# A conv FFN on one core: loads, squares and conversions put at other steps of the down projection

## The reference, cut to what matters

```python
h = rms_norm(x, norm_ffn)
up = causal_dwconv(h @ ffn_w_up, ffn_conv_w, ffn_conv_b)      # 1024 -> 2 * 2816
u_val, u_gate = jnp.split(up, 2, axis=-1)
x = x + (jax.nn.gelu(u_gate) * u_val) @ ffn_w_down            # 2816 -> 1024
return rms_norm(x, norm_final)
```

## Time and profile before

| what | value |
|---|---|
| time, median of 3 runs | 2558.03 us (2553.03 to 2568.3) |
| profiled execution, device time | 2553.03 us |
| its span, first to last instruction | 2551.2 us |
| TensorE busy | 2426.0 us (95%), 11968 matmuls |
| VectorE, ScalarE, GpSimd busy | 1709.5, 1129.2, 983.1 us |
| mean granted TensorE clock | 0.972 of full speed |

### The profile page before, as it was taken

One profiled execution on the slowest core, in us unless ns is written; L12 is line 12 of the kernel. 1 busy time (PEld: TensorE's weight loads), 2 busy tenths in 40 slices (PEclk: granted clock), 3 DMA queues, 4 the chain that ended last, 5 costly groups with the idle time before them and its releaser, 6 DMA issues.

```text
span 2551.2 us, 33398 instructions
## 1 busy us (share of the span) xinstructions
PE 2426.0 (95%) x11968; PEld 1944.2 (76%) x11968; DVE 1709.5 (67%) x2323; ACT 1129.2 (44%) x2008; POOL 983.1 (39%) x784
## 2 busy tenths in 40 slices
PE   6999999999899996997799999999899999999997
PEld 5777878777678875785688888878777888787886
DVE  6554547775255675352788878768987888886755
ACT  6534254332146654321544454444564444444444
POOL 4111003432056773131555655413434655551311
PEclk9999999899899998998899999999999999999999
DMA  4333325442497424544432232378642322326764
GB/s 161 103 99 104 101 75 162 141 149 91 157 309 257 131 64 147 197 148 163 166 117 107 108 114 109 116 248 275 197 142 109 114 95 108 120 90 209 247 194 160
DMA packets 189445, 376.60 MB, mean 148 GB/s; under 512 B 17105, under 2 KB 61153, under 8 KB 180193
## 3 DMA queue, kind: packets, MB, share of 16 engines
q1 hardware_dynamic: 189280, 374.47, 43.3%
HBM read 250.43 MB, written 123.98 MB: 147 GB/s over the span
## 4 chain that ended last, share of the span: by engine, by line
PE 42%; DVE 6%; issue 1%; ACT 1%; DMA 1%; POOL 0%; SPq 0%; ACTq 0%; DVEq 0%; POOLq 0%
PE ff_bank L2107 14%; PE ff_bank L2109 14%; PE ff_bank L2108 14%; DVE ff_y_gate L2804 2%; DVE ff_ring L2817 1%; DMA ff_raw_ring<-a_t 1%; DVE ff_ring L2765 1%; DVE ff_b_lo L2759 1%; ACT ff_y_gate L2618 0%; DMA ff_b_raw<-h_t 0%; DVE ff_u L2786 0%; ACT ff_e L2597 0%; DVE ff_u L2788 0%; ACT ff_ring L2633 0%; POOL ffn_rstd L2517 0%
## 5 line engine op out<-in xcount | busy, mean ns | idle before, releaser
L2107 PE MATMUL ff_bank<-ff_b_hi,ff_ring 128*128 128x512 f32 x1232 | 486.4, 395 | 32.9 <-DVE ff_b_lo L2759 13.0
L2108 PE MATMUL ff_bank<-ff_b_lo,ff_ring 128*128 128x512 f32 x1232 | 482.3, 391 | 0.0
L2109 PE MATMUL ff_bank<-ff_b_hi,ff_ring 128*128 128x512 f32 x1232 | 482.1, 391 | 0.0
L2817 DVE TENSOR_TENSOR ff_ring<-ff_raw_ring,ff_ring 128x512 fp32r<-128x512 f32 x308 | 248.1, 852 | 114.1 <-ACT ff_ring L2633 114.0
L66 PE MATMUL ip_bank<-ip_x_hi,ip_w_hi 128*128 128x512 f32 x736 | 303.6, 413 | 17.6 <-DVE ip_x_lo L701 16.5
L2107 PEld LDWEIGHTS ff_bank<-ff_b_hi,ff_ring 128*128 128x128 f32 x1232 | 233.0, 189 | 95.9 <-issue 44.9
L67 PE MATMUL ip_bank<-ip_x_lo,ip_w_hi 128*128 128x512 f32 x736 | 294.6, 400 | 0.0
L68 PE MATMUL ip_bank<-ip_x_hi,ip_w_lo 128*128 128x512 f32 x736 | 293.5, 399 | 0.0
L2109 PEld LDWEIGHTS ff_bank<-ff_b_hi,ff_ring 128*128 128x128 f32 x1232 | 233.0, 189 | 49.4
L2108 PEld LDWEIGHTS ff_bank<-ff_b_lo,ff_ring 128*128 128x128 f32 x1232 | 233.1, 189 | 47.8 <-issue 0.2
L2633 ACT ACTIVATE ff_ring<-ff_raw_ring 128x512 fp32r<-128x512 f32 x308 | 177.0, 623 | 198.7 <-PE ff_bank L2109 95.1
(11 more groups left out here) (263 smaller groups left out, 4655.4 us busy)
## 6 DMA issues: line engine op xcount, KB each, us to landing
ff_raw<-in_slabs SPq DMA_DIRECT2D x43, 1024.0 KB, 4.8
proj_t<-ip_staged SPq DMA_DIRECT2D x92, 256.0 KB, 2.6
a_t<-ff_y_val SPq DMA_DIRECT2D x44, 512.0 KB, 2.6
t_t<-ff_t_sum SPq DMA_DIRECT2D x88, 256.0 KB, 2.0
ff_raw_ring<-s_t SPq DMA_DIRECT2D x88, 256.0 KB, 3.2
ff_raw_ring<-t_t SPq DMA_DIRECT2D x88, 256.0 KB, 3.8
ff_raw_ring<-in_w_down SPq DMA_DIRECT2D x66, 256.0 KB, 3.2
ff_raw_ring<-a_t SPq DMA_DIRECT2D x66, 256.0 KB, 4.3
```

The lines of the kernel that those rows point to most:

```text
L2107: pe.matmul(out, w_hi, x_hi, start=first, stop=False, skip_group_check=resumed)
L2108: pe.matmul(out, w_hi, x_lo, start=False, stop=False, skip_group_check=resumed)
L2109: return pe.matmul(out, w_lo, x_hi, start=False, stop=last, skip_group_check=resumed)
L2817: dve.tensor_tensor(ring[:, to, 1, :], raw_ring[:, raw_slot(half, n), i, :], ring[:, to, 0, :].bitcast(F32), ALU.subtract).then_inc(d_lo_r ...
```

## The change

It computes the same and moves work of the down stage to other steps:

- `load_x` stands at steps 10 to 25 in place of 14 to 29, and `load_piece` at 26 to 41 in place of 30 to 45.
- At the start of the stage, ScalarE does `tap` of the last pair's value before `high_step(3)`, and VectorE does `convolve` and `multiply` of it before `low_step(3)` and `low_step(4)`.
- `square` 0 to 3 stand at steps 44 to 47 in place of 56 to 59, and 4 to 7 at 60 to 63 in place of 62 to 65. `high_b` begins at step 46 in place of 48.
- `norm_b` is done four at a time after steps 33, 37, 41 and 45, in place of one after each of the steps 36 to 51.
- GpSimd does the slab sums for the next up stage before `totals` 12 to 15, in place of after.

```diff
--- before.py
+++ after.py
@@ -2408,10 +2408,10 @@
                     if n == 8:
                         store_a(half, PAIRS - 1)
                         store_t(half, PAIRS - 1)
-                    if 14 <= n < 30:
-                        load_x(half, n - 14)
-                    if half == 0 and 30 <= n < 46:
-                        load_piece(1, n - 30)
+                    if 10 <= n < 26:
+                        load_x(half, n - 10)
+                    if half == 0 and 26 <= n < 42:
+                        load_piece(1, n - 26)
                     if half == 0 and n in (50, 56):
                         load_slab(1, (n - 50) // 6)
                 store_out(half, 1)
@@ -2551,9 +2551,10 @@
                     sums_of_slab(1, 0)
                 totals(half, range(OC, 3 * OC))
                 if half == 0:
-                    totals(half, range(3 * OC, 4 * OC))
                     last_sum_of_slab(1, 0)
                     sums_of_slab(1, 1)
+                if half == 0:
+                    totals(half, range(3 * OC, 4 * OC))
 
         @block.scalar
         def _(act):
@@ -2702,23 +2703,22 @@
                     gelu(half, g)
                     high_next(6)
                 high_step(half, 2)
-                high_step(half, 3)
                 tap(half, PAIRS - 1, 0)
-                for n in range(4, STEPS):
+                for n in range(3, STEPS):
                     if n == KP + 3:
                         keep_first_product(half)
-                    if 56 <= n < 60:
-                        square(half, n - 56)
-                    if 62 <= n < 66:
-                        square(half, n - 62 + OC)
+                    if 44 <= n < 48:
+                        square(half, n - 44)
+                    if 60 <= n < 64:
+                        square(half, n - 60 + OC)
                     if n == 70:
                         for t in range(2 * OC, 3 * OC):
                             square(half, t)
                     if n == 73:
                         root(half, 1)
                     high_step(half, n)
-                    if half == 0 and 48 <= n < 48 + 28:
-                        high_b(1, n - 48)
+                    if half == 0 and 46 <= n < 46 + 28:
+                        high_b(1, n - 46)
                 if half == 0:
                     for m in range(8):
                         high_w(1, m)
@@ -2877,16 +2877,15 @@
                     low_next(6)
                     move(half, g, 3)
                 low_step(half, 2)
-                low_step(half, 3)
                 convolve(half, PAIRS - 1, 0)
-                low_step(half, 4)
                 multiply(half, PAIRS - 1)
-                for n in range(5, STEPS):
+                for n in range(3, STEPS):
                     if n % KP == 3 and 2 <= n // KP <= 6:
                         drain(half, n // KP - 2)
                     low_step(half, n)
-                    if half == 0 and 36 <= n < 52:
-                        norm_b(n - 36)
+                    if half == 0 and 33 <= n < 49 and n % 4 == 1:
+                        for i in range(4):
+                            norm_b(n - 33 + i)
                     if half == 0 and n >= 49:
                         low_b(1, n - 49)
                     if n >= 73:
```

## The result

The changed kernel takes 2576.88 us (median of 12 runs, 2570.05 to 2581.57), the kernel before 2559.84 (12 runs on the same chip, 2553.03 to 2568.3). The ratio is 1.0061, 95% interval 1.0046 to 1.0078: slower by 16 to 17 us, where 2557.5 and no change were predicted. The time lies outside the predicted range too.

A forecast was written before the change was run, and what follows sets the result against it. TensorE bounds the kernel (busy 2426 of 2551 us). Terms -0.2 - 0.9 + 0.4 = -0.7 on the profiled 2553.0 give about 2552.3; the median lies 5.0 higher: 2557.5, range 2549 to 2567 for 8 in 10.

The forecast's parts named there:

- The start of a down stage: Start of both down stages, new `tap`, `convolve`, `multiply` order and earlier loads: together -0.2 us, from -1.8 to +4.5.
- The wait at step 3: TensorE at step 3 of a down stage: new wait of 2.9 us, plus 2.4 for the clock.
- it pays for something that came later anyway: Down stage start: the new wait is offset at step 11, which waits for the copy; net 1.0 us less, first half.
- Rival B: Down stage start not paid back, if `load_x` delays step 13's transfer by 3 us or more: 2566 us, 14%.
- The middle: Middle of the first down stage: -9.9 + 6.1 + 2.4 + 0.5 = -0.9 us, from -3.1 to +4.3.
- The old waits: First down stage, TensorE's waits at steps 52, 53 and 58 with their clock loss: all gone, -9.9 us.
- Eight sums on GpSimd: Before step 46: two sums beside scalings and six alone, 3.4 + 7.5 = 10.9 us, then a copy of 0.98.
- over at step 45: First down stage: scalings finished at step 45, no sum left when `low_b` begins at 49; last batch's first scaling ends 1778.0.
- the upper bound of 8.8: TensorE's wait at step 46, predicted 6.1 us, if all sums take the contended 1.68; 5.0 if all run alone.
- The end: Slab sums ahead of totals 12 to 15 before the next up stage: net +0.4 us, from 0 to 3.
- Rival A: No stop at step 46: middle of the first down stage -9 us in all, 2549 us, 8%.
- Rival C: Lead lost at step 46 not rebuilt; TensorE waits twice more, 3 + 3.4 each: 12.8 us on top, 2570, 12%.

The follow-up runs named there:

- The swap back: Changed kernel with GpSimd's totals 12 to 15 ahead of the slab sums again; ratio to the kernel before 1.0056.
- all three parts undone: Changed kernel with squares at old steps, `norm_b` one at a time after steps 30 to 45, and old start order; ratio to the kernel before 1.0001.

## Why the prediction was wrong, point by point

**The start of a down stage: predicted -0.2 for both halves, measured about +2.2 and +3.4.** The wait at step 3 was foreseen, its size was 4.0 and not 2.9. The step that failed is "it pays for something that came later anyway". The copy's start was put at +35.0, the +34.0 of before and 1 us for the `load_x` transfers; it came at +37.9. By the runs, the start order alone puts it at +36.7. The other 1.2 us may be the loads, less by their transfers than by the wait of `load_x` 0 in SyncE's queue, as the load of step 11 leaves at +26.6 after and at +24.3 with only the new order; in the second half the loads add nothing (step 11 at +38.5 and +38.7). The prediction had seen the reason and booked it too low: "the load of step 6 now waits for the low parts of step 3, 5 us later than before, and eats it" was set only against the gain of the earlier stores. With three slots the load of step 6 passes its delay on to steps 9 and 12 and that of step 7 to steps 10 and 13, and the conversion of step 13 stands ahead of the copy. Of the 6.0 us at step 6, 3.9 are left there; how much of them came by the slots and how much by the stores between the loads of steps 8 and 9 no run separates. The estimate took the transfer of step 13 as a fixed moment of the trace before, though it is itself at the end of the chain that the change delays. Rival B (the start isn't paid back) came true, with 9 us in all forecast and 5.6 measured, but by this chain and hardly by the `load_x` transfers to which it was put down.

**The middle: predicted -0.9, measured +10.4.** Its parts:

- The old waits were to go, -9.9. They went down to 0.87 and 1.16 without a clock loss: -7.9. This part was nearly right, though one reason given for it was not (the slab sums met low parts at step 58 and no drain), and with the scalings one at a time at early steps, in the kernel before, the waits at steps 52 and 53 go as well, so the batch wasn't needed for it.
- Eight sums on GpSimd from the last batch on: predicted 10.9 us, measured from 1798.67 to 1809.86, 11.2. Right. The copy took 0.60, not 0.98.
- The moment at which they begin: the last batch was put at 1778.0, +123.7; it began at 1797.85, +133.3. This is the step that failed in the middle. The prediction took the scalings as "over at step 45" and put no cost on the batches ahead of the last. The first indeed costs none; the second and the third take 2.1 us more beside their sums, the low parts behind them 2.2 more, and these make the slots late.
- TensorE wanted step 46 at +131.9 by the prediction, and at +140.1 by the trace (8.2 later, from the start and the waits at steps 38 and 42 with their clock). The low parts were ready at +149.6 and not +138.0, 11.6 later: 9.6 by the start of the batch, 0.8 as the first sum waits for the first scaling (1797.85 to 1798.67), 1.1 as the last pair of low parts takes 2.37 beside the `totals` and not 1.28. The difference, 3.4, is the 9.53 that stands where 6.1 was predicted; the upper bound of 8.8 was too low as well.
- New waits altogether: 0.57 + 3.27 + 9.53 = 13.4, and 4.0 for the clock behind the last two, counted from matmuls 0.43 us apart and more in place of 0.227: 17.4. With -7.9 that is +9.5 of the 10.4.

On VectorE a batch of four is 2.73 us alone and 4.8 with sums beside it, and the six low parts behind are 5.83 for 3.6. Together that is 4.3 us for four sums of 6.8 us in all: 1.1 us for each sum, as in the pair of the earlier trace rows. The prediction used that row for GpSimd's side (how long the eight sums take), and not for VectorE's. The rule of the Trainium skill weighed there (SBUF — State Buffer, section "SBUF: two separate sides", VectorE with two SBUF inputs and GpSimd lock one another out) spoke against exactly this batch, and the trace agrees with it better than the prediction said. That held the 1.1 us against the 1.68 of a sum beside VectorE, but such a sum takes 1.3 alone, so 0.4 of the 1.68 is time that the sum itself loses. The pair of the earlier trace rows is one low part of 0.68 and one of 1.78 that ends 0.6 us, about its own length alone, after the sum does (1779.26 and 1778.70). That is what taking turns would look like; the 1.1 us are 0.2 short of a sum's 1.3.

**The end: predicted +0.4 with 0 to 3, measured +1.5.** The totals came 4.2 us later and not 1.6. The slab sums could start 3.0 us ahead of the first square (1907.99), near the 3.7 counted on. The step that failed is their length: 7.3 us in place of 5.5, since the first one lies beside a row of five low parts (1904.26, 3.09 us) and takes 3.50 where a sum alone takes 1.3:

```profile
1905.02 3.50 POOL L2461 TENSOR_TENSOR ff_raw<-ff_raw,ff_s 128x512 f32<-128x512 f32 x1 [21.91 <-DVE ff_ring L2765]
```

The 2.65 behind them went, as said. The swap back gave nothing, so within what can be measured the term is right.

**Rival A** (no stop) didn't come. **Rival C** (lead not rebuilt after step 46) is the one on the right side, but not by its mechanism: behind step 46 only 0.87 and 1.16 are lost. The lead was lost ahead of step 46. "I am wrong if step 11 still waits 2 us or more" was one of the signs; the first half shows 1.59, the second 2.45.

**The chances.** The sum itself has a slip of 0.2 us (2552.3 and 5.0 are 2557.3, not 2557.5), which changes nothing. Of the bounds of -4.9 to +11.8 the prediction said that they will not all fall on one side. They did, and their upper end was still 6 us short of the 17.9. They weren't independent: one loop (slot, transfer, conversion, low part, slot) carries each delay into the next term. 6% for slower rested on them.

## What to carry to other kernels

Before an instruction is moved later in a queue, ask what buffer it frees and follow that buffer once around its ring: a transfer in the trace before is no fixed moment when its own issue hangs on what is moved. Work put in a batch on one engine, each piece of which releases work on an engine that slows it, puts the whole cost of it in front of one step. Spread out it costs no less in all: of the twelve sums that the scalings release, ten cost VectorE about 1.1 us each in both forms (one by one, in nine pairs of 2.38 and a scaling of 1.78). But one by one no step carries more than one sum, while behind the third batch the low parts of step 42 end 8.1 us after those of step 41 (1783.8 to 1791.9), and three steps of TensorE are 8.2. And a square that waits for a sum far back in another queue is to be put no earlier than that queue comes to it, as all that stands behind it waits too.

## What the runs showed of the hardware

- VectorE loses about 1.1 us for each GpSimd sum that falls between its low parts or scalings: a pair of low parts 1.28 to 2.38, step 3's pair 2.4, a batch of four scalings 2.73 to 4.8, a batch and six low parts together 4.3 for four sums. It isn't so everywhere. A drain, which reads PSUM, takes 2.47 with a sum of 1.31 beside it (1782.80 in the earlier trace rows, 1782.96 in the earlier trace rows), so neither loses anything. And beside five low parts in a row (1904.26, after) VectorE loses nothing, at 0.6 us each, while GpSimd's sum takes 3.50. Which of the two engines goes first in such a case, the runs don't say.
- What is untouched by the change isn't constant. The FFN's first matmul starts between 1212.9 and 1231.0 us over the profiled executions, with the same code in front of it. The second down stage takes 234.1 to 238.2 with the same code, while the wait of 4.0 at step 3 was the same to 0.01 us in every trace that has it. The difference between two spans is thus a poor measure of a change of 0.5%; stage by stage from a common matmul it is a better one.
- What a wait costs by the clock isn't given by its length. With all three parts undone, TensorE waits 3.06 us at step 11 of the second half and the granted clock behind it stays at 1.00, while in the same trace it is 0.91 over the 20 us from 1688, behind the 3.05 of the first half; with only the batches, it waits 2.06 after an earlier 2.90 and comes back at the lower level, 0.91 over 20 us. The windows of the one and of the other (columns as in the earlier trace rows):

```profile
2350.00:2370.00 20.00, 17.70 (x78) 14.72 (x79) 13.50 (x16) 10.65 (x20) 6.40 (x4) 1.00 0.83 282
```

```profile
1815.00:1835.00 20.00, 16.60 (x65) 12.88 (x64) 16.51 (x21) 11.75 (x22) 9.62 (x8) 0.91 0.64 203
```
